# Pairs prepared before the substitution, and two feed-forward units on the residual before its norm

## The reference

```python
def rwkv7_scan(r, decay, k, v, kk, a):              # per head, S is 64 x 64
    sa = einsum('bhij,bhj->bhi', S, -kk_t)
    S = S * w_t + sa[..., None] * (kk_t * a_t) + v_t[..., None] * k_t
    y_t = einsum('bhij,bhj->bhi', S, r_t)
...
def _conv_ffn(x, norm_ffn_g, w_up, conv_ffn_w, w_down):
    h = _rmsnorm(x, norm_ffn_g)
    u = _causal_dwconv(h @ w_up, conv_ffn_w)         # 3 taps, 2 x 2816 channels
    gt, up = jnp.split(u, 2, axis=-1)
    return (jax.nn.silu(gt) * up) @ w_down
```

## Time and profile before

| | us |
|---|---|
| median of 3 runs | 1470.88 (1470.73 to 1476.52) |
| the profiled execution | 1469.24 |
| its span, first to last instruction | 1467.4 |
| busy PE / DVE / ACT / POOL | 1408.8 / 933.8 / 487.7 / 487.6 |
| mean granted clock of PE | 0.982 |

### The profile page before, as it was taken

One profiled execution on the slowest core, in us unless ns is written; L12 is line 12 of the kernel. 1 busy time (PEld: TensorE's weight loads), 2 busy tenths in 40 slices (PEclk: granted clock), 3 DMA queues, 4 the chain that ended last, 5 costly groups with the idle time before them and its releaser, 6 DMA issues.

```text
span 1467.4 us, 18610 instructions
## 1 busy us (share of the span) xinstructions
PE 1408.8 (96%) x7612; PEld 1144.1 (78%) x7612; DVE 933.8 (64%) x1322; ACT 487.7 (33%) x663; POOL 487.6 (33%) x131
## 2 busy tenths in 40 slices
PE   7999978699998999999999999999989999999997
PEld 6778646587888877888888887878878888888886
DVE  6679868735413357769969974762457888885122
ACT  5443367243324232122222223322233333332121
POOL 0004110012535323343434433334423443443441
PEclk9999999799999999999999999999989999999999
DMA  6221000023314211232232231222222223222221
GB/s 206 87 87 58 29 2 2 4 85 118 129 71 144 87 58 58 86 100 102 86 105 97 87 115 58 86 98 104 86 87 86 87 88 113 87 99 95 84 96 58
DMA packets 21349, 125.14 MB, mean 85 GB/s; under 512 B 2384, under 2 KB 3408, under 8 KB 7696
## 3 DMA queue, kind: packets, MB, share of 16 engines
q1 hardware_dynamic: 20752, 121.71, 23.6%
q10 hardware_dynamic: 512, 2.23, 0.4%
HBM read 121.84 MB, written 2.10 MB: 84 GB/s over the span
## 4 chain that ended last, share of the span: by engine, by line
PE 88%; DVE 8%; ACT 3%; issue 1%; DMA 0%; DVEq 0%; SPq 0%; ACTq 0%
PE bank L402 25%; PE bank L404 24%; PE bank L403 24%; PE bank L1008 1%; PE bank L1024 1%; PE bank L354 1%; DVE conv_b L2406 1%; PE bank L393 1%; ACT prob L1409 1%; PE bank L877 1%; PE bank L958 1%; PE bank L626 0%; ACT probT L1415 0%; PE bank L362 0%; DVE op_hi L1736 0%
## 5 line engine op out<-in xcount | busy, mean ns | idle before, releaser
L1204 POOL TENSOR_TENSOR w_lo<-w_raw,w_hi 128x2048 fp32r<-128x2048 f32 (+1 forms) x102 | 468.2, 4590 | 762.8 <-ACT w_hi L1256 746.9
L402 PE MATMUL bank<-op_hi,w_hi 128*128 128x512 f32 x1344 | 529.8, 394 | 6.4 <-DVE op_lo L1758 2.3
L404 PE MATMUL bank<-op_hi,w_lo 128*128 128x512 f32 x1344 | 525.9, 391 | 0.0
L403 PE MATMUL bank<-op_lo,w_hi 128*128 128x512 f32 x1344 | 525.9, 391 | 0.0
L402 PEld LDWEIGHTS bank<-op_hi,w_hi 128*128 128x128 f32 x1344 | 253.6, 189 | 63.7 <-issue 6.3
L404 PEld LDWEIGHTS bank<-op_hi,w_lo 128*128 128x128 f32 x1344 | 253.3, 188 | 54.6
L403 PEld LDWEIGHTS bank<-op_lo,w_hi 128*128 128x128 f32 x1344 | 253.4, 189 | 54.0 <-issue 0.7
L1256 ACT ACTIVATE w_hi<-w_raw 128x2048 fp32r<-128x2048 f32 (+2 forms) x109 | 205.6, 1887 | 265.3 <-PE bank L404 265.3
L2299 DVE SCALAR_TENSOR_TENSOR bank<-pad_b,par,bank 128x512 f32<-128x512 f32 x232 | 175.3, 756 | 7.8
L2465 DVE TENSOR_TENSOR tmp<-tmp,conv_f 128x512 f32<-128x512 f32 x22 | 101.6, 4617 | 16.4 <-ACT tmp L1682 16.4
L2196 DVE TENSOR_TENSOR x_res<-bank,x_res 128x512 f32<-128x512 f32 x24 | 16.5, 691 | 136.9 <-PE bank L404 136.8
(11 more groups left out here) (374 smaller groups left out, 1702.0 us busy)
## 6 DMA issues: line engine op xcount, KB each, us to landing
w_raw<-in_w_units SPq DMA_DIRECT2D x104, 1024.0 KB, 4.9
w_raw<-in_w_units SPq DMA_DIRECT2D x4, 768.0 KB, 4.2
x_res<-in_x SPq DMA_DIRECT2D x8, 256.0 KB, 6.5
x_res<-in_x ACTq DMA_DIRECT2D x2, 1024.0 KB, 6.3
out<-x_res SPq DMA_DIRECT2D x8, 256.0 KB, 2.2
w_raw<-in_w_units SPq DMA_DIRECT2D x3, 512.0 KB, 9.0
w_raw<-in_w_units SPq DMA_DIRECT2D x4, 256.0 KB, 5.6
mem_tok<-in_mem SPq DMA_DIRECT2D x1, 1024.0 KB, 5.2
```

The source lines that it names most:

```text
L402: nc.tensor.matmul(b[:, 0:width], h, xh[:, x0 + k, 0:width], start=start and k == ks[0], stop=False)
L403: nc.tensor.matmul(b[:, 0:width], h, xl(x0 + k, width), start=False, stop=False)
L404: mm = nc.tensor.matmul(b[:, 0:width], l, xh[:, x0 + k, 0:width], start=False, stop=stop and k == ks[-1])
L1204: nc.gpsimd.tensor_tensor(w_lo[u % 2][:, 0:nk, :], w_raw[u % 2][:, 0:nk, :], w_hi[u % 2][:, 0:nk, :].bitcast(F32), ALU.subtract).then_inc( ...
```

## The change

In the pairs' part the four lists are rewritten. The scan's preparations of the pairs 1 to 3 come earlier, with a second pair of buffers (`prep_odd`) for odd pairs, so that the blocks of all pairs are made before the third pair's scores. DVE's substitution is cut at steps 4, 10, 16 and 24, and `heads_out`, the last `maxima` and `probs` stand between the pieces, `heads_out(3)` behind `blocks_out`. PE has `heads_out(3)` before `token_major(1)`. The grams of chunks 0 and 1 are copied by ACT and masked by POOL (`grams_masked`), and PE waits for the mask.

In the feed-forward the units `up` 0 and 1 multiply the split of x_res times the gain alone (plain_hi by ACT, plain_lo by DVE, made chunk by chunk behind the residual); the token sums and the spread are issued within unit 0, and DVE multiplies the results of these two units by 1/rms in PSUM before the taps. From unit 2 on the normed operand is used as before. ACT's list has the weight splits of units 2 and 3 in front of the taps of unit 0.

```diff
@@ -121,6 +121,7 @@
...
+PLAIN_UNITS = 2
...
         prep = [at(f"prep{j}", R0 + 59392 + 2080 * j, [4 * 129 + 4]) for j in range(4)]
...
         sq_f = at("sq_f", R0, [CH, T])
+        plain_hi = at("plain_hi", R0 + 16384, [CH, T], F32R)
...
         ps = [ctx.enter_context(nc.psum_tensor(f"bank{b}", [P, T], F32)) for b in range(BANKS)]
+
+        def decay_home(i, j):
+            return prep_odd[j][:, 0:T] if i % 2 else prep[j][:, 0:T]
 
...
@@ -676,8 +683,11 @@
             def value_products(c, i2):
                 v = tok_v[c % 2]
                 heads = [(NI * odd + i, P * i + HD * odd, odd, i - 2 * i2) for i in (2 * i2, 2 * i2 + 1) for odd in range(2)]
-                for odd in range(2):
-                    evacuated(pe, ("gk", c, odd, i2))
+                if c < 2:
+                    pe.wait_ge(sem("gram_masked"), 4 * c + 2 * i2 + 2)
+                else:
+                    for odd in range(2):
+                        evacuated(pe, ("gk", c, odd, i2))
                 b = bank(("xv", c, i2))
                 for h, f, odd, n in heads:
                     o = 128 * odd + HD * n
...
             scores(0)
-            strict_upper(0)
+            key_bonus(1)
+            decay_and_rate(2)
+            norms_spread(2)
             head_values()
-            key_bonus(1)
-            for p in range(1, NI):
-                head_inputs(p)
-                scores(p)
-                if p + 1 < NI:
-                    decay_and_rate(p + 1)
-                    norms_spread(p + 1)
-                strict_upper(p)
-                if p + 1 < NI:
-                    probabilities_turned(p - 1)
-                    heads_out(p - 1)
-                    key_bonus(p + 1)
+            head_inputs(1)
+            key_bonus(2)
+            strict_upper(1)
+            scores(1)
+            decay_and_rate(3)
+            norms_spread(3)
+            probabilities_turned(0)
+            strict_upper(2)
+            key_bonus(3)
+            head_inputs(2)
+            strict_upper(3)
+            scores(2)
+            heads_out(0)
+            probabilities_turned(1)
+            heads_out(1)
+            head_inputs(3)
+            scores(3)
 
             def chunk_values(c, before_second=None):
                 evacuated(pe, ("tv", c))
...
@@ -798,9 +816,9 @@
             heads_out(NI - 2)
             chunk_values(0)
             probabilities_turned(NI - 1)
+            heads_out(NI - 1)
             token_major(1)
             value_grams(1)
-            heads_out(NI - 1)
             chunk_values(1)
             pe.wait_ge(sem("blocks_out"), 2)
             side_products(0)
...
@@ -1074,11 +1092,20 @@
             gated(1)
             for i in range(4):
                 unit_tiles("wo2", i, merged_hi, plain(merged_lo), ready=None if i else "merged_ready")
-            token_sums("f", sq_f)
-            pe.wait_ge(sem("tok_f_ready"), 1)
-            spread("rs_f", tok_rs)
-            for i in range(FC):
-                unit_tiles("up", i, oh, ol, ready=None if i else "ffn_ready")
+
+            def statistics(k):
+                pe.wait_ge(sem("plain_ready"), k + 1)
+                if k == 3:
+                    token_sums("f", sq_f)
+                elif k == CH - 1:
+                    pe.wait_ge(sem("tok_f_ready"), 1)
+                    spread("rs_f", tok_rs)
+
+            unit_tiles("up", 0, plain_hi, plain(plain_lo), ready=statistics)
+            for i in range(1, PLAIN_UNITS):
+                unit_tiles("up", i, plain_hi, plain(plain_lo))
+            for i in range(PLAIN_UNITS, FC):
+                unit_tiles("up", i, oh, ol, ready=None if i > PLAIN_UNITS else "ffn_ready")
             for i in range(4):
                 bs = None
                 for k0 in (0, 8, 16):
...
             nc.gpsimd.memset(invT[quarter(0), :, quarter(1)], 0.0).then_inc(sem("zeroed"), 1)
+
+            def grams_masked(c):
+                for i2 in range(2):
+                    for odd in range(2):
+                        h = NI * odd + 2 * i2
+                        evacuated(pool, ("gk", c, odd, i2))
+                        g = g_k[:, h:h + 2, :, :]
+                        nc.gpsimd.affine_select(out=g, in_=g, compare_op=ALU.is_ge, fill=0.0, base=-1,
+                                                pattern=[[0, 2], [1, 2], [1, P]], channel_multiplier=-1).then_inc(sem("gram_masked"), 1)
+
+            grams_masked(0)
+            grams_masked(1)
             filled(pool, ("o", NI - 1))
...
@@ -1368,16 +1407,23 @@
                 u += 1
                 split_hi(u + 1)
             def decay_and_rate(i):
+                if i >= 2:
+                    act.wait_ge(sem("prep_ready"), i - 1)
+                    act.wait_ge(sem("bk_decayed"), 2 * i - 2)
+                elif i == 1:
+                    filled(act, ("ga", 1, 1))
+                evac(A(decay_home(i, 0), take(act, ("z", i))[:, :], ACT.Tanh, scale=0.5, bias=half_wa[:, i:i + 1]), ("z", i))
+                evac(A(decay_home(i, 1), take(act, ("a", i))[:, :], ACT.Tanh, scale=0.5, bias=half_wa[:, NI + i:NI + i + 1]), ("a", i))
+                evacuated(act, ("a", i))
+                if i:
+                    act.wait_ge(sem("rk_ready"), i)
+                A(rs[:, :], decay_home(i, 1), ACT.Identity, scale=half_ka[:, i:i + 1], bias=omka[:, i:i + 1]).then_inc(sem("rate_ready"), 1)
+
+            def decays(i):
+                act.wait_ge(sem("cum_ready"), i + 1)
                 if i:
                     act.wait_ge(sem("prep_ready"), i)
                     act.wait_ge(sem("bk_decayed"), 2 * i)
-                evac(A(prep[0][:, 0:T], take(act, ("z", i))[:, :], ACT.Tanh, scale=0.5, bias=half_wa[:, i:i + 1]), ("z", i))
-                evac(A(prep[1][:, 0:T], take(act, ("a", i))[:, :], ACT.Tanh, scale=0.5, bias=half_wa[:, NI + i:NI + i + 1]), ("a", i))
-                evacuated(act, ("a", i))
-                A(rs[:, :], prep[1][:, 0:T], ACT.Identity, scale=half_ka[:, i:i + 1], bias=omka[:, i:i + 1]).then_inc(sem("rate_ready"), 1)
-
-            def decays(i):
-                act.wait_ge(sem("cum_ready"), i + 1)
                 A(tmp[0][:, 0:516], prep[2][:, 0:516], ACT.Exp, scale=-0.5 * KAPPA).then_inc(sem("exps"), 1)
                 A(tmp[1][:, 0:516], prep[2][:, 0:516], ACT.Exp, scale=0.5 * KAPPA).then_inc(sem("exps"), 1)
 
...
             decay_and_rate(1)
+            decays(1)
             strict_upper(0)
-            decays(1)
+            decay_and_rate(2)
+            exps(0)
+            decays(2)
             head_values()
-            exps(0)
-            for p in range(1, NI):
-                head_inputs(p)
-                if p + 1 < NI:
-                    decay_and_rate(p + 1)
-                strict_upper(p)
-                if p + 1 < NI:
-                    turned(p - 1)
-                    decays(p + 1)
-                    exps(p)
+            head_inputs(1)
+            strict_upper(1)
+            decay_and_rate(3)
+            turned(0)
+            decays(3)
+            strict_upper(2)
+            exps(1)
+            head_inputs(2)
+            strict_upper(3)
+            turned(1)
+            exps(2)
+            head_inputs(3)
+
+            def value_grams(c):
+                for i2 in range(2):
+                    if c:
+                        filled(act, ("yv", c - 1, i2))
+                    for odd in range(2):
...
+                        b = take(act, ("gk", c, odd, i2))[:, :].rearrange("p (n a t) -> p n a t", n=2, a=2)
+                        evac(A(g_k[:, h:h + 2, :, :], b, ACT.Copy), ("gk", c, odd, i2))
 
             def value_products(c, i2):
                 b = take(act, ("xv", c, i2))[:, 0:256].rearrange("p (o n) -> p o n", o=2)
@@ -1462,6 +1522,7 @@
 
             token_major(0)
             turned(NI - 2)
+            value_grams(0)
...
             chunk_values(0)
             turned(NI - 1)
             token_major(1)
...
@@ -1667,17 +1729,24 @@
                     A(misc[:, 127:128], ones[:, 0:1], ACT.Sqrt)
                 for c in (2 * i, 2 * i + 1):
                     evacuated(act, ("wo2", i, c % 2))
+                    A(plain_hi[:, c, :], x_res[:, c, :], ACT.Copy, scale=pcol("norm_ffn_g_2", c)).then_inc(sem("plain_hi"), 1)
                     A(sq_f[:, c, :], x_res[:, c, :], ACT.Square).then_inc(sem("sq_f"), 1)
             root(tok_rs, "tok_f_ready")
+            after_unit()
             hi_chunks((0, CH), "ffn")
+            for i in range(1, PLAIN_UNITS):
+                after_unit()
             for i in range(FC):
                 for m in range(2):
                     if i >= 2:
                         act.wait_ge(sem("act_ready"), i - 1)
+                    if i < PLAIN_UNITS:
+                        act.wait_ge(sem("up_scaled"), 2 * i + m + 1)
 
                     A(conv_f[i % 2][m][:, 0:T], take(act, ("up", i, m))[:, :], ACT.Copy,
                       scale=pcol("conv_ffn_w_2", 4 * FC + FC * m + i)).then_inc(sem("tap_ready"), 1)
```

(67 more changed lines are left out.)

9 lines of the change are left out of this document (7 added, 2 removed).

## The result

The changed kernel is slower. Its ratio to the kernel before is 1.0026, 95% interval 1.0016 to 1.0037: 3.8 us more on the median shown before, where 4.3 us less was forecast, and outside the range given. Medians of 20 runs each: 1476.20 us after, 1470.75 before. The 20 runs of the changed kernel lie in two groups, nine from 1471.73 to 1473.96 and eleven from 1476.08 to 1479.02, and the profiled one (1477.59, span 1475.8) is of the upper, that of before (1469.24) among its kernel's faster ones; so the two traces side by side overstate the loss, the medians do too, and the halves of the change are read from ratios beside the traces.

A forecast was written before the change was run, and what follows sets the result against it. PE, busy 1408.8 of 1467.4 us, was taken to bound the kernel, so only its stops or half clock could give time back. 7.6 - 3.3 = 4.3 us faster: 1466.6 us for the median, range 1459.5 to 1472.8.

The forecast's parts named there:

- the fourth bank of `value_grams(1)`: Pairs: PE stops there 7.7 us, from 258.8 to 266.5, until DVE's heads_out(3) frees the bank of ("o",3).
- unit 2's second bank: Feed-forward: ring of 7 banks, so PE stands 9.1 us before up unit 2 until DVE's taps of (0,0) free it.
- B: Rival, feed-forward: the bank of up0 m0 is no wait; 7.6 + 1.2 us faster, 1462.0; 12%.
- D: Rival, pairs: the bank of ("o",3) is no wait, side_products starts at blocks_out; 13.3 - 3.3, 1460.9; 9%.
- C: Rival, unit 2: POOL's w_lo holds the taps, bank 4.3 us later, Part 2 -7.6; slower, 1473.0; 12%.
- the half clock behind the new stop: Pairs: costs 2.0 us before side_products (273.5); from there the old half clock is mostly gone, 2.7 us gained.
- The price at full clock: Pairs: 1.0 + 3.8 + 0.3 us from the stop to side_products; 6.1 for side_products, token_major(2) and value_grams(2).
- part 1: Pairs first, outputs between substitution steps: +7.6 us, from 5 to 11; side_products 4.9 sooner, 2.7 more behind it.
- The masks' hold: Pairs: POOL's masks of 0.8 us hold DVE's substitution, 1.4 us for the first four and 1.2 later, 2.4 rounded.
- rival E: Pairs' part gives nothing: PE's stops among the pairs bring half clock, blocks_out some 7 us later; near 1472; 7%.
- Part 2: Feed-forward, two up units on the residual: gap after wo2 closed but new stop before unit 2; -3.3 us, -6 to -1.5.
- All that follows moves along: Behind the pairs, up to the next phase: everything, DMA of mem_2 and the phase's weights included, shifts with the gain.

The follow-up runs named there:

- ring8: Changed kernel with CONV_BANK put back into the ring before up: 0.9996 of the kernel before, 4.4 us faster than the changed kernel.
- heads_early: Changed kernel with DVE's heads_out(3) between steps 26 and 27 of the substitution: 0.9967 of the kernel before, 8.7 us faster than the changed kernel.
- filler7: Changed kernel with 7 useless matmuls in PE's stop before the fourth bank of value_grams(1): 0.9970 of the kernel before, 8.2 us faster than the changed kernel.
- ffn_only: Kernel before with the feed-forward's half of the change alone: 1.0018 of the kernel before, 2.6 us slower.
- pairs_only: Kernel before with the pairs' half of the change alone, feed-forward as before: 0.9987 of the kernel before, 1.9 us faster, not told from no change.
- ring8_whi: ring8 with ACT's w_hi of unit 4 before the taps of unit 1, later ones a unit ahead: 0.9962 of the kernel before, 5.0 us faster than ring8.
- combo2: ring8_whi and heads_early together, but DVE's heads_out(0) behind blocks_in, substitution steps 0 to 16 before heads_out(1), heads_out(3) directly before blocks_out: 0.9903 of the kernel before.

## Why the prediction was wrong

**What held.** Both new waits are where the prediction put them and released by whom it said: the fourth bank of `value_grams(1)` by DVE's `heads_out` (7.7 us forecast, 6.0 measured), and unit 2's second bank by the taps (9.1 and 8.8). `ring8` and `heads_early` take away the bank alone and with it the wait, so rivals B and D, that these are no waits, fall. The Trainium skill's remark that consistent bubbles can mean PSUM ran out ("Trainium Kernel Development and Optimization", Best Practices) fits `ring8`, where one bank more took away 8.8 us, though that was a single stop and no repeated one. A mask was put at 0.8 us and took 0.79 beside the substitution; two in a row took 1.23 us once the substitution was over. The taps were not held by POOL (1.53 us for two) so C's mechanism fell too, though the time came out above C's. That 9.1 and 8.8 lie so near is in part luck: counted from the end of `wo2`, PE came to this stop 1.65 us later than forecast, by half clock in unit 0, and the bank came free 1.1 us later, with a product by 1/rms of 0.70 us in front of the taps that the prediction had put at nothing.

**The step that failed** is the half clock behind the new stop. The prediction reads "I take 2.0 and have `side_products` at 273.5", and next that the half clock on `side_products`, `token_major(2)` and `value_grams(2)` "is mostly gone", 2.7 us more. Measured: from the fourth bank to `side_products` 8.8 us against 4.8 in `filler7`, so 4.0 and not 2.0; and from there to `side_blocks` 9.04 us, where before has 8.75 and `filler7` 5.53, so 0.3 lost and not 2.7 gained. The prediction took the return of the clock, 3.8 to 7.4 us after the work, from two other places, where other work stood behind the stop. Behind this one it took 16.8 us. What stayed where it was is the place in the program: in all seven traces in which the clock is at half when `side_products` starts (before, `ffn_only`, the changed kernel, `pairs_only`, `ring8`, `ring8_whi`, `combo2`) the clock comes back 0.8 to 1.8 us after the start of `value_grams(2)`. An earlier start of PE therefore lengthened the stretch at half clock instead of leaving it behind. Why the clock comes back there and not sooner stays open. The price at full clock was right: `filler7` takes 4.8 us for the 5.0 of the first part and 5.5 for the 6.1 of the second.

**The sum of part 1**, forecast against measured at `side_blocks`: PE goes on at 268.19 and not 266.5, 1.7 us; 8.8 us and not 7.0 to `side_products`, 1.8; no gain behind it, 3.0. Of the forecast 7.6 us that leaves 1.15, which is what the trace has (287.15 to 286.00); `pairs_only` measures 1.9 by its ratio. The first 1.7 us are a size too: DVE waits 17.7 us in all and not 13.0. Its waits for the pairs' scores are as forecast, 10.0 for 10.5; the rest is mostly this row of its waits:

```profile
DVE gate_a L2097 <- PE bank L640: 4.6, 2, 3.8
```

PE was late with `heads_out(1)`, after its 3.2 us for the bank of ("o", 0), and then ran it at half clock:

```profile
228.82 4.54 PE L633 MATMUL bank<-probT,v_tok 128*64 128x512 f32 x16 [0.88 <-ACT probT L1461]
```

Two pairs later the same row takes 2.38. This is rival E's mechanism, which had 7% and no term in the sum. The masks' hold was 1.0 us, from three instructions at 0.74, and not 2.4: the second four ran when the substitution was over.

**Part 2** was -3.3 forecast. Its trace says -4.2 and its ratio -2.6 (-5.0 to -0.4). The difference in the trace is the 1.65 us of half clock in unit 0, which no step had; unit 2 lost 2.3 where 2.6 stood.

**"All that follows moves along"** failed as well. In the profiled execution 13.7 us ran at 0.50 behind the next stop, where before had 3.4 us; `ffn_only` shows that this is not of the change.

**The sign.** With part 1 at 1.2 to 1.9 and part 2 at -2.6 to -4.2 the sum is between -0.7 and -3.0 us; measured is -3.8 (-5.4 to -2.4). Forecast was +4.3, and most of the turn is in part 1.
